# Two output projections and the panels behind them: accumulator banks exchanged, one weight split placed earlier

## What is computed

```python
def first_block(x, p, ...):
    h = x
    for i in range(2):
        hn = rmsnorm(h, mix_norm[i])
        if i % 2 == 0:
            h = h + mixer_ab(hn, ...)      # ends in concat([o_a, o_b]) @ ab_w_out   ("wo0")
        else:
            h = h + mixer_c(hn, ...)       # starts with q, k, v = split(hn @ c_w_in), ends in o @ c_w_out ("wo1")
        h = h + conv_glu_ffn(rmsnorm(h, ffn_norm[i]), ffn_up[i], ...)
        gate = jax.nn.sigmoid(rmsnorm(h, ple_norm[i]) @ ple_gate[i])
        h = h + gate * (p[i] @ ple_proj[i])
    return h
```

## Time and profile before

| | us |
|---|---|
| median of 3 runs | 1050.41 |
| lowest and highest | 1049.27 and 1051.16 |
| the profiled execution | 1049.21 |
| its span in the profile | 1047.5 |
| PE busy | 995.0 (95%) |
| DVE busy | 705.5 (67%) |
| ACT busy | 570.2 (54%) |

### The profile page before, as it was taken

One profiled execution on the slowest core, in us unless ns is written; L12 is line 12 of the kernel. 1 busy time (PEld: TensorE's weight loads), 2 busy tenths in 40 slices (PEclk: granted clock), 3 DMA queues, 4 the chain that ended last, 5 costly groups with the idle time before them and its releaser, 6 DMA issues.

```text
span 1047.5 us, 16427 instructions
## 1 busy us (share of the span) xinstructions
PE 995.0 (95%) x6658; PEld 909.1 (87%) x6658; DVE 705.5 (67%) x1011; ACT 570.2 (54%) x800; POOL 135.7 (13%) x124
## 2 busy tenths in 40 slices
PE   6998798999999989989899999999999999999996
PEld 6987687999998878777899998888988889999995
DVE  5787755888883574965788888456564566954654
ACT  6735544666563385676565665346574466443432
POOL 4002511243320000000023332000100000000000
PEclk9999998999999999999999999999999999999999
DMA  9553215786656563414676664665645553465541
GB/s 319 178 176 106 81 41 135 206 255 197 186 165 227 183 227 124 148 55 121 174 199 174 188 183 168 212 201 161 203 156 161 161 158 125 160 197 168 201 141 41
DMA packets 165643, 174.38 MB, mean 166 GB/s; under 512 B 4094, under 2 KB 132592, under 8 KB 165568
## 3 DMA queue, kind: packets, MB, share of 16 engines
q1 hardware_dynamic: 163376, 167.92, 51.2%
q0 software_dynamic: 2160, 5.41, 1.7%
q10 hardware_dynamic: 32, 0.01, 0.0%
HBM read 172.25 MB, written 1.07 MB: 165 GB/s over the span
## 4 chain that ended last, share of the span: by engine, by line
PE 74%; ACT 9%; DVE 9%; issue 5%; DMA 2%; POOL 1%; SPq 0%; POOLq 0%; ACTq 0%; DVEq 0%
PE bank L811 36%; PE bank L792 18%; PE bank L830 12%; PE bank L846 4%; ACT w_hi L1143 3%; DVE w_lo L1446 2%; DMA w_raw<-in_ab_w_in 2%; PE bank L875 1%; ACT le_s L1371 1%; ACT le L1242 1%; DVE prod L1523 1%; POOL sp__80 L659 1%; ACT L1242 0%; DVE ex L1500 0%; DVE exb L1500 0%
## 5 line engine op out<-in xcount | busy, mean ns | idle before, releaser
L1446 DVE TENSOR_TENSOR w_lo<-w_raw,w_hi 128x2048 fp32r<-128x2048 f32 x157 | 358.7, 2289 | 186.7 <-ACT w_hi L1143 186.7
L1143 ACT ACTIVATE w_hi<-w_raw 128x2048 fp32r<-128x2048 f32 x157 | 299.8, 1914 | 259.1 <-PE bank L811 146.0
L811 PE MATMUL bank<-x_hi,w_hi 128*128 128x256 f32 x912 | 260.1, 285 | 2.9 <-issue 2.6
L811 PE MATMUL bank<-x_lo,w_hi 128*128 128x256 f32 x912 | 258.0, 283 | 0.0
L811 PE MATMUL bank<-x_hi,w_lo 128*128 128x256 f32 x912 | 258.0, 283 | 0.0
L811 PEld LDWEIGHTS bank<-x_hi,w_hi 128*128 128x128 f32 x912 | 174.9, 192 | 4.3 <-issue 3.3
L811 PEld LDWEIGHTS bank<-x_lo,w_hi 128*128 128x128 f32 x912 | 175.0, 192 | 0.2
L811 PEld LDWEIGHTS bank<-x_hi,w_lo 128*128 128x128 f32 x912 | 174.9, 192 | 0.0
L792 PE MATMUL bank<-w_hi,x_hi 128*128 128x512 f32 x256 | 102.9, 402 | 8.2 <-issue 4.0
L811 PE MATMUL bank<-y_hi,w_hi 128*128 128x256 f32 x352 | 99.6, 283 | 3.9 <-issue 3.9
L668 POOL TENSOR_TENSOR gf<-sgate,cc 128x256 f32<-128x256 f32 x44 | 82.1, 1866 | 162.0 <-ACT sgate L1164 161.9
(11 more groups left out here) (339 smaller groups left out, 1586.7 us busy)
## 6 DMA issues: line engine op xcount, KB each, us to landing
w_raw<-in_ffn_up SPq DMA_DIRECT2D x88, 512.0 KB, 5.2
w_raw<-in_w_in SPq DMA_DIRECT2D x35, 1024.0 KB, 5.3
w_raw<-in_ffn_down SPq DMA_DIRECT2D x22, 1024.0 KB, 5.0
w_raw<-in_ab_w_in SPq DMA_DIRECT2D x14, 1024.0 KB, 5.3
w_raw<-in_ple_gate SPq DMA_DIRECT2D x8, 1024.0 KB, 5.1
w_raw<-in_c_w_in SPq DMA_DIRECT2D x6, 1024.0 KB, 5.2
w_raw<-in_ab_w_out SPq DMA_DIRECT2D x4, 1024.0 KB, 5.1
w_raw<-in_w_mem_kv SPq DMA_DIRECT2D x4, 1024.0 KB, 5.4
```

Source lines behind the costliest of these rows:

```text
L811: mm = pe.matmul(bank[b][:, c * 256:c * 256 + 256], wv[w][:, k, c * P:(c + 1) * P], x[:, k, :], start=(k == 0 and m == 0 and not (first an ...
L1143: act.activation(whi[n % RING][:, :], raw[n % RAW][:, :], ACT.Copy).then_inc(*mark("weights_hi", ("hi", n)))
L1446: dve.tensor_tensor(wlo[n % RING][:, :], raw[n % RAW][:, :], plain(whi[n % RING][:, :]), ALU.subtract).then_inc(*mark("weights_lo", ("lo", ...
```

## The change

Three edits. `wo0` puts block 0 in banks 6 and 7 and block 1 in 4 and 5. `kv` moves from banks 6 and 7 to 4 and 5, block 0 of `qs` from 4 and 5 to 6 and 7, and block 1 of `qs` from 6 and 7 to 4 and 5. In `wo0` and `wo1` the split of the next stage's second panel (19 or 71) stands directly behind the third panel, ahead of the square of block 0 and turns 0 and 1. No instruction is added or taken away.

```diff
@@ producer, in schedule()
             if first + i == block_done(stage, 0):
+                if stage in HALVES_FIRST:
+                    out.append(("split", first + 2 + RING))
                 out.append(("square", k, 0))
                 if stage in HALVES_FIRST:
-                    out.extend([("turn", k, 0), ("turn", k, 1), ("split", first + 2 + RING)])
+                    out.extend([("turn", k, 0), ("turn", k, 1)])
@@ wide_bank
             if stage == "wo0":
-                return 4 + 2 * block + t
+                return 6 - 2 * block + t
+            if stage in ("kv", "qs"):
+                return 6 - 2 * (WIDE_BLOCK[stage, block] % 2) + t
```

## The result

| | before | after |
|---|---|---|
| median | 1049.84 us (1049.23 to 1051.16, 4 runs) | 1036.51 us (1035.17 to 1037.04, 4 runs) |
| the profiled execution | 1049.21 us | 1036.46 us |
| its span | 1047.5 us | 1034.7 us |
| mean granted clock of TensorE | 0.989 | 0.991 |

The changed kernel takes 0.9869 of the time before (95% interval 0.9852 to 0.9887), 13.3 us less by the medians. The four runs of before are the three shown above and one more.

A forecast was written before the change was run, and what follows sets the result against it. PE was busy 995.0 of 1047.5 us, so only its gaps could be won: 6.2 (A) + 4.4 (C) + 2.8 (B) = 13.4 us, from 1050.4 to 1037.0 us; range 1034.5 to 1041.5.

The forecast's parts named there:

- A: Between `wo0` and `up0`, panel 18 waits for block 1's residual, late behind panel 19's split; gain 6.2 us.
- the full-clock share: At A, TensorE's clock no longer falls after the gap; 2.1 us.
- the wait behind the banks: At A, panel 18's first 12 matmuls run during the wait for the residual; 1.3 us.
- the split: At A, moving panel 19's split ahead brings block 1's residual forward; 2.8 us.
- B: Between `wo1` and `up1`, turns 2 and 3 wait for a residual queued behind panel 71's split; gain 2.8 us.
- C: Between `gate0` and `kv`, `kv` waits for bank 6, held by block 1's addition, and the clock falls; gain 4.4 us.
- What the new banks hold up: At `mv` and the first block of `wo0`, reused banks cost 0; `mv` has 1.9 us to spare, `wo0` bound 0.4 us.
- Gains kept downstream: Behind A, C and B, pacing by PE or chains from its results keeps the gains, which add to 13.4 us.
- Rival 1: The clock's 3.8 us do not come back, falls being at other gaps or absent in most runs before; 1040.8 us, chance 0.12.
- Rival 2: Most runs before also had a clock fall at B, 1.8 us more to win; 1035.2 us, chance 0.06.
- Rival 4: Late loads of panels 19 or 71 hold ACT's queue behind the moved splits; slower than before, L = 18 gives 1054.4 us, chance 0.02.

The follow-up runs named there:

- the filled gaps: The kernel before, plus matmuls with unread results in two PE gaps, 16 ahead of panel 18 and 11 ahead of `kv`: 1047.86 us, ratio 0.9984.
- the `kv` banks: The kernel before with only the banks of `kv` and `qs` exchanged: 1045.29 us, ratio 0.9961 to before.

## Why the prediction was right, point by point

Forecast 1037.0 us and a gain of 13.4; measured 1036.51 and 13.3. The three places gave what the sum said, each to 0.1 us. That the medians agree as closely is in part luck: 22 executions of before spread over 4.7 us, the medians here are of four each, and in the profiles 0.5 us were lost again ahead of panel 16.

- **A, 6.2 us.** Measured 6.1. Taking out the 0.5 us by which the stretch starts later, the steps stand where they were put: `w_hi` at 160.62 (160.1), `w_lo` 162.57 (162.1), residual ended 167.63 (167.4), turns 168.14 (167.67), the k = 4 matmul 170.66 (170.22). Its three terms are confirmed separately: the full-clock share by the filled gaps (1.9 in place of 2.1), the wait behind the banks by the split alone (1.1 us remain to be won: 0.87 idle and the steps behind it; the text said 1.3), the split by the bank edits alone (2.7 us remain: 6.1 - 3.4; the text said 2.8). The statement that neither edit alone has the whole is borne out.
- **B, 2.8 us.** Measured 2.8, with the turns 1.42 us behind panel 70's first matmul. The bank edits alone left it as it was, gap and all.
- **C, 4.4 us.** Measured 4.4. The turns start 2.92 us behind `kv` (2.87 by the text), right after the addition.
- **What the new banks hold up, 0 us.** Measured 0. The changed kernel at `mv`, ACT's second reading and then PE:

```profile
421.21 0.69 ACT L1210 ACTIVATE qk<-bank,small 128x512 f32<-128x512 f32 x1 [2.02 <-PE bank L796]
422.15 1.94 PE L1019 MATMUL bank<-ident,qkn 128*128 128x128 f32 x16 [0.98 <-DVE qkn L1772]
423.84 0.47 PE L796 MATMUL bank<-w_hi,x_hi 128*128 128x512 f32 x1
```

  The reading is over at 421.90 and `mv` starts at 423.84, behind the transposes: 1.94 us to spare, as in the earlier trace rows. `wo0` in its new banks loses nothing either: from the first matmul of panel 14 to the first of panel 16 it takes 13.28 us in both traces (141.06 to 154.34 and 141.56 to 154.84).
- **Gains kept downstream.** The segments between the places are equal to 0.1 us (the sums of the table meet the spans), except for what the clock does.
- **Rival 1, the clock.** It did not decide here, but the working gave it a condition that was too loose and a chance that was too low for what it is. Of the four gaps beyond 2.5 us in this part (A, B, C and `mk`) the changed kernel has one left, and that one had no fall in its profile, so 13.3 us came through; the other three executions have mean clocks of 0.991 to 0.993, no lower than its 0.991. Where gaps are left, falls there can take back what was won: 3.9 of 7.8 us with the bank edits alone, 1.1 of 5.1 with the `kv` banks. I had put it as one thing that happens or not (3.8 us, 0.12); it is a cost that can appear at each remaining gap. My expectations for these two partial kernels left out a fall at `mk` or B, and for the first that was the miss. The Trainium skill, "TensorE: Matmul & The Clock Gate", Part 1 (The HAM clock gate), says that the number of slow matmuls of one kernel varies from run to run because the monitor's phase is not tied to the kernel's start. The runs here agree in so far as the 22 executions of before have mean granted clocks from 0.986 to 0.991; no trace shows the monitor itself.
- **Rival 2, a fall at B in most runs before.** It was priced at C's 1.8 us. The two traces with such a fall behind B's 2.63 us gap show 1.1 and 1.2 us.
- **Rival 4, late loads.** Its mechanism and its remoteness are both confirmed, its break-even was mis-sized. By the text A turns to a loss beyond a landing time of 15.8 us, so 16.3 us should have cost A 0.5 us against before; it cost 27.85 - 25.60 = 2.25. The term left out is the clock: the new gap of 6.11 us brought a fall, which the row of 174 to 176 shows at 0.50, and the text had booked the clock's 2.1 us as won. The excess is 1.75 us.

What stays open: how often each gap had a fall in the executions without a trace, in before and in the filled kernel, and what decides it.

## What to carry to other kernels

When the last reader of a bank is the latest step of the stage before, let the next stage start in a bank whose reader is early; it costs a line and here gave 4.4 us. On an in-order engine put the long step that is ready early (a split whose buffers are free) into the idle time ahead of the steps that are not ready yet, and look at what would happen if it were late after all: here 16.4 us in place of 7.1, with a load some 10 us later than any seen in that stretch. Judge a partial edit by the length of its own segment in the trace as well as by the median, since half-clock stretches at other gaps can hide or fake several microseconds.

## What the runs showed of the hardware

- **The clock falls at some gaps of one length and not at others.** In the ten traces half clock came behind one of eight gaps of 2.61 to 2.62 us at `mk`, behind two of four of 2.63 us at B, behind all three of 2.75 us at C, not behind the one of 2.54 us at A, and behind all six of 3.9 us and more at A and B. Length alone does not settle it: ahead of panel 16, in before, the clock was at half from 83.1 to 86.6 us right behind a gap of 2.32 us.
- **What a fall costs** depends on how long it lasts and on what PE does in it. Two that lasted 6.8 us cost 2.7 us in `mk` (256 columns wide, 0.21 us from one matmul to the next in place of 0.12) and 2.1 us at A; those that lasted 3.4 us cost 1.8 us at C (512 columns wide), some 1.5 us at A (0.7 less than the long one) and 1.1 to 1.2 us at B. At A and B PE also waits for the turns' round trip, which may be why it costs less there; that was not tested.
- **Multiplying instead of waiting kept the clock full** at both places, for 16 and 11 matmuls of 0.23 us, and made the program 1.8 us faster by the medians (ratio 0.9972 to 0.9995) without removing any work. Removing the gaps is worth more: in the traces 10.5 us at the same two places, against 3.5.
- **The same work ahead of panel 16** (only the banks of panels 14 and 15 differ in some kernels) ended between 152.45 and 155.07 us in ten profiles, with half clock in different stretches between 80 and 136 us. That alone is 2.6 us of spread between executions.
